# Hyena layer: both directions' filters on halves of the array, squares summed on GpSimd, filters placed among another round's products

## The reference, cut to what matters

```
def hyena_filters(length, w1, b1, f1, w2, b2, f2, w3):
    ...
    hid = jnp.sin(f1 * (feats @ w1 + b1))
    hid = jnp.sin(f2 * (hid @ w2 + b2))
    h = (hid @ w3).astype(jnp.float32).reshape(length, HY_ORDER, HY_DIRS, HY_W)
    h = h * jnp.exp(-t * decay)[:, None, None, :]
    return h * lax.rsqrt(jnp.sum(h * h, axis=0, keepdims=True) + EPS)

def hyena_layer(...):
    p = h @ w_in
    u = dwconv(p[..., :3 * HY_W], conv_w)
    v, x1, x2 = jnp.split(u, 3, axis=-1)
    filt = hyena_filters(...)
    z = x1 * long_conv(v, filt[:, 0, 0], filt[:, 0, 1], skip[0])
    y = x2 * long_conv(z, filt[:, 1, 0], filt[:, 1, 1], skip[1])
```

## Time and profile before

| | |
|---|---|
| runs | 4025.53 us median of 3 (4020.6 to 4029.58) |
| profiled execution, span | 4026.6 us, 72398 instructions |
| profiled execution beside the median | 1.1 us above it; the page gives no other time of its own |
| PE busy | 3681.6 us, 91% |
| DVE / ACT / POOL busy | 1654.0 / 1184.3 / 1366.7 us |
| Hyena rounds in the trace | 824.7 to 1319.8 us |

### The profile page before, as it was taken

The page is one execution under the profiler, slowest core; times in us unless marked ns, Lnnn a source line. Parts: engine busy times, 40 slices in busy tenths (PEclk is TensorE's granted clock), DMA queues, the critical chain, the costliest instruction groups (busy, mean ns, idle before and its releaser), DMA issues.

```text
span 4026.6 us, 72398 instructions
## 1 busy us (share of the span) xinstructions
PE 3681.6 (91%) x31788; PEld 2339.7 (58%) x31788; DVE 1654.0 (41%) x2930; ACT 1184.3 (29%) x2153; POOL 1366.7 (34%) x1215
## 2 busy tenths in 40 slices
PE   8997878999999998898899999899888888889998
PEld 3754565434444455565455555445666776748887
DVE  1345343234434122444433333643565656533344
ACT  3253222222212264432300000211556666420002
POOL 1320442002112022657433323334343434225444
PEclk9998787988898999989999999999999999989999
DMA  5430000621001211540111111132000000022222
GB/s 198 148 100 21 2 2 11 211 86 33 29 28 43 84 47 63 189 161 18 52 53 62 62 54 55 60 123 75 36 16 19 25 16 4 14 84 95 84 84 74
DMA packets 196419, 263.77 MB, mean 66 GB/s; under 512 B 6119, under 2 KB 151655, under 8 KB 194056
## 3 DMA queue, kind: packets, MB, share of 16 engines
q1 hardware_dynamic: 189024, 241.74, 18.0%
q10 hardware_dynamic: 7080, 17.40, 1.1%
HBM read 246.53 MB, written 12.58 MB: 64 GB/s over the span
## 4 chain that ended last, share of the span: by engine, by line
PE 50%; ACT 5%; DVE 4%; issue 3%; POOL 1%; DMA 0%; ACTq 0%; DVEq 0%; SPq 0%; POOLq 0%
PE ps L238 40%; PE ps L3123 2%; PE ps L771 2%; ACT mem L848 1%; PE ps L382 1%; PE ps L798 1%; PE ps L786 1%; PE ps L489 1%; DVE mem L829 1%; PE ps L3642 1%; POOL mem L3425 0%; PE ps L3650 0%; ACT mem L858 0%; PE ps L498 0%; ACT mem L3058 0%
## 5 line engine op out<-in xcount | busy, mean ns | idle before, releaser
L238 PE MATMUL ps<-mem 64*64 64x64 f32 (+4 forms) x25184 | 2690.3, 302 | 155.4 <-POOL mem L3026 29.0
L238 PEld LDWEIGHTS ps<-mem 64*64 64x64 f32 (+1 forms) x25184 | 1742.8, 155 | 1111.1 <-issue 578.2
L3026 POOL TENSOR_TENSOR mem<-mem 128x256 f32<-128x256 f32 (+1 forms) x264 | 226.0, 868 | 357.9 <-ACT mem L3535 178.8
L866 POOL TENSOR_SCALAR mem<-mem 128x768 f32<-128x768 f32 (+2 forms) x128 | 219.0, 1723 | 197.6 <-DVE mem L832 197.6
L2267 ACT ACTIVATE mem<-ps 128x384 f32<-128x384 f32 (+1 forms) x80 | 35.6, 445 | 781.1 <-PE ps L238 738.8
L2254 POOL TENSOR_TENSOR mem<-mem 128x512 f32<-128x512 f32 (+1 forms) x80 | 100.2, 1252 | 443.2 <-PE ps L238 371.2
L596 POOL TENSOR_TENSOR mem<-mem 128x512 f32<-128x512 f32 (+1 forms) x72 | 75.2, 1060 | 431.7 <-ACT mem L591 428.6
L2278 DVE TENSOR_TENSOR mem<-mem,ps 128x384 f32<-128x384 f32 (+1 forms) x80 | 39.9, 499 | 417.3 <-PE ps L238 417.3
L3123 PE MATMUL ps<-mem 128*128 128x128 f32 x960 | 178.1, 303 | 31.2 <-DVE mem L3048 20.1
L3056 ACT ACTIVATE mem<-ps 128x256 f32<-128x256 f32 (+1 forms) x220 | 101.4, 461 | 200.0 <-PE ps L3123 199.5
L3048 DVE TENSOR_TENSOR mem<-mem,ps 128x256 f32<-128x256 f32 (+1 forms) x220 | 109.7, 514 | 122.7 <-PE ps L238 121.9
(11 more groups left out here) (336 smaller groups left out, 4126.9 us busy)
## 6 DMA issues: line engine op xcount, KB each, us to landing
mem<-i_mod_w SPq DMA_DIRECT2D x48, 1024.0 KB, 6.8
mem<-i_ffn_wg SPq DMA_DIRECT2D x22, 1024.0 KB, 5.1
mem<-i_ffn_wu SPq DMA_DIRECT2D x22, 1024.0 KB, 5.1
mem<-i_e_w_in SPq DMA_DIRECT2D x16, 1024.0 KB, 6.0
mem<-i_o_w_in SPq DMA_DIRECT2D x16, 1024.0 KB, 5.5
mem<-i_ffn_wd SPq DMA_DIRECT2D x16, 1024.0 KB, 5.2
mem<-i_e_mod_w SPq DMA_DIRECT2D x12, 1024.0 KB, 11.8
mem<-i_o_mod_w SPq DMA_DIRECT2D x12, 1024.0 KB, 6.9
```

The lines of the kernel that those rows point to most:

```text
L238: ins = e.h.matmul(out, l, r, start=(i == 0), stop=(i == n - 1))
L866: K.pool.h.tensor_scalar(w, w, stat(i, o, 1), None, MUL).then_inc(*nm.up(tag, i, o))
L3026: K.pool.h.tensor_tensor(m3(self.slot(l)), self.lraw, bm(C(K, f"cm{self.d}", l, 64), 2 * self.np), MUL).then_inc(*self.mk.up(key, l))
```

## The change

Filters of both directions are computed as a pair: the second layer of the filter network writes `h2` on 128 partitions (its weights are loaded twice side by side), the w3 of both directions lies on the two halves of the partitions of one tile `w3t`, and the two products of a pair use rows 0 to 63 and 64 to 127 of the array and two banks. The host lays w3 out so. `w3t` is `K.rows[1]`, outside the ring; the filters H are moved out of Y (to the end of memory and to the part of `yo` that is written last), so that they can be computed while Y is in use. The squares go to G, POOL adds the four blocks, and one product with ones per direction is left. Norm, sum and difference are done in two halves z. A round's filters are computed in the round before, in four steps tt. The spectra, turns and copies are written in another order on PE and ACT.

```
-        self.w = [m[0:33, 0:64], m[0:64, 64:128]]
+        self.w = [m[0:33, 0:64], m[0:64, 64:192]]
+        self.rows = [64, 128]
...
+    w3t = K.rows[1]
-    H = [Y[:, 0:4, :], Y[:, 4:8, :]]
+    H = [K.mem[:, MEM - 2048:MEM].rearrange("p (a b) -> p a b", b=512), yo[:, 4:8, :]]
+    sums_at = lambda it: 0 if it else 2
+    place = lambda tt, d: 2 * ((tt + 1) % 2) + d
+    spectrum = lambda f, c: 2 * ((f + 1) % 2) + c
...
+    def filters_pe(it, tt):
+        if tt == 0:
+            window[it], _ = K.take(kn(256))
+            K.spent(window[it], fl, it, 3, 1)
+            K.pe.wait_ge(*sa.at(1))
+            K.pe.wait_ge(*lw.at(it))
+        for d in range(2):
+            vacant(K, place(tt, d))
+        for d in range(2):
+            ins = K.pe.h.matmul(K.ps[place(tt, d)], h2[64 * d:64 * d + 64, tt * 128:tt * 128 + 128], w3t[64 * d:64 * d + 64, :], start=True, stop=True)
+            K.busy[place(tt, d)] = [(fl, (it, tt, d))]
+        ins.then_inc(*w3.up(it, tt))
...
+    def filters_pool(it):
+        for tt in range(1, 4):
+            for d in range(2):
+                K.pool.wait_ge(*sqr.at(it, tt, d))
+                if tt > 1:
+                    K.pool.wait_ge(*ad.at("squares", it, tt - 1, d))
+                K.pool.h.tensor_tensor(G[:, 4 * d, :], G[:, 4 * d, :], G[:, 4 * d + tt, :], ADD).then_inc(*ad.up("squares", it, tt, d))
+    def sums_pe(it):
+        for d in range(2):
+            vacant(K, 2 + d)
+            K.pe.wait_ge(*ad.at("squares", it, 3, d))
+            K.pe.h.matmul(K.ps[2 + d], C(K, "ones"), G[:, 4 * d, :], start=True, stop=True).then_inc(*ss.up(it, d))
...
+    def norms_dve(it):
+        for z in range(2):
+            for d in range(2):
+                K.dve.wait_ge(*sqr.at(it, "r", d))
...
+                h = H[d][:, 2 * z:2 * z + 2, :]
+                K.dve.h.tensor_tensor(h, h, bm(G[:, 4 * d + 1, :], 2), MUL).then_inc(*fl.up(it, "n", d, z))
+    def sums_pool(it):
+        for z in range(2):
...
+            K.pool.h.tensor_tensor(HS[:, part, :], H[0][:, part, :], H[1][:, part, :], ADD).then_inc(*hs.up(it, z))
...
+        for tt in range(4):
+            filters_pe(0, tt)
+        for it, hf, o in rounds:
+            for x, t in enumerate(early[it]):
+                if x == sums_at(it):
+                    sums_pe(it)
+                conv_pe(it, t)
+            products(it, 0)
+            products(it, 1)
+            turned(it, 0)
+            turned(it, 1)
+            products(it, 2)
+            turned(it, 2)
+            turned(it, 3)
+            products(it, 3)
+            forward(it)
+            ahead = (lambda tt: filters_pe(it + 1, tt)) if it < 3 else (lambda tt: None)
+            ahead(0)
+            conv_pe(it, ("x", 2))
+            ahead(1)
+            inverse(it, 0, 1)
+            ahead(2)
+            conv_pe(it, ("x", 3))
+            ahead(3)
+            inverse(it, 2)
+            inverse(it, 3)
...
+            K.sp.wait_ge(*(w3.at(it - 1, 3) if it else K.sig("mod_turn", "pe").at("mod_b0", 20)))
+            K.sp.h.dma_start(w3t, I["w3"][:, o, hf * 512:hf * 512 + 512]).then_inc(*lw.up(it, by=16))
```

More of the change, by code:

```diff
@@ L1946, in long_convolutions @@
     rounds = [(hf * 2 + o, hf, o) for hf in range(2) for o in range(2)]
[L1947 to L1950, removed]
+    early = {it: ([("u", j) for j in range(4)] if o == 0 else []) + [("x", 0), ("x", 1)] for it, hf, o in rounds}
     order = {}
     for it, hf, o in rounds:
-        for part in tiles[it]:
-            for t in part:
-                order[it, t] = len(order)
+        for t in early[it] + [("x", 2), ("x", 3)]:
+            order[it, t] = len(order)
@@ new lines, in conv_pe, with conv_act @@
+    def conv_pe(it, t):
+        c = order[it, t]
+        b = 4 + c % 2
+        if t[1] % 2 == 0:
+            cur[0:2] = K.take(kn(256))
+        n, s = cur
+        vacant(K, b)
+        group(K.pe, K.ps[b], ((s[:, k, (t[1] % 2) * 128:(t[1] % 2) * 128 + 128], hap(k, 0, NX)) for k in range(KT)), KT).then_inc(*lin.up("hc", c))
+        K.busy[b] = [(pd, (c,))]
+        if t[1] % 2:
+            K.spent(n, lin, "hc", c)
+    def conv_act(it, t):
+        c = order[it, t]
+        K.act.wait_ge(*zero.at(1))
+        K.act.wait_ge(*lin.at("hc", c))
+        if c >= 2:
+            K.act.wait_ge(*cv.at(c - 2, 2))
+        K.act.h.activation(pad[c % 2][:, 1:NX + 1], K.ps[4 + c % 2], ACT.Copy).then_inc(*pd.up(c))
@@ L2067, in pe, with turned, forward @@
+        def turned(it, j):
+            b = 2 + j % 2
+            vacant(K, b)
+            K.pe.wait_ge(*fo.at(it, j, 1))
+            for i in range(4):
+                ins = K.pe.h.transpose(K.ps[b][:, i * 128:(i + 1) * 128], fold[j % 2][:, i * 128:(i + 1) * 128], C(K, "ident"))
+            ins.then_inc(*tu.up(it, j))
+            K.busy[b] = [(ut, (it, j))]
+        def forward(it):
             K.pe.wait_ge(*ut.at(it, 3))
@@ new lines, in inverse @@
+        def inverse(it, *js):
+            for j in js:
+                vacant(K, 6 + j % 2)
+            for i in range(2):
+                for f in range(4):
+                    c = i ^ odd(f)
+                    K.pe.wait_ge(*ad.at(it, f, c))
+                    for j in js:
+                        ins = K.pe.h.matmul(K.ps[6 + j % 2][:, 256 * i:256 * i + 256], Y[:, 4 * c + f, j * 128:(j + 1) * 128], Fi[:, c, f, :], start=f == 0, stop=f == 3)
+                        if f == 3 and i:
+                            ins.then_inc(*iv.up(it, j))
+                            K.busy[6 + j % 2] = [(mx, (it, j, 1))]
```

375 lines of the change are left out of this document (175 added, 200 removed).

## The result

| | before | after |
|---|---|---|
| runs of the comparison, median | 4023.07 us of 4 | 3899.56 us of 4 (3895.11 to 3903.02) |
| ratio | | 0.9698, 95% interval 0.9681 to 0.9715 |
| profiled span | 4026.6 | 3901.6 |
| the Hyena rounds, first filter product to first gate product | 495.04 | 373.96 |

What follows compares the result with a forecast made beforehand. TensorE (PE) was taken to bound the kernel, busy 3681.6 of 4026.6 us. The terms take the Hyena layer from 495.1 to 381.1 us, 114 less, giving a median of 3911.5 (forecast 3911); range 3896 to 3938.

Steps and rivals of the forecast that it cites:

- Step 1: Four filter stages, one ahead of each Hyena round, leave PE's path, with the slab's DMA wait: -124.8 us.
- Step 2: First round's filters still stand alone with nothing to hide them; first convolution at 836.5: +11.8 us.
- Step 3: Rounds 1 to 3: 12 filter pairs among other products, 1.0 us each plus two row-count changes of 0.2: +17 us.
- 4 ones-products: Since POOL sums the squares, 32 ones-products become 8, at 0.86 us each: +7 us.
- Step 5: PE's waits at turns, copies and inverse go, -15 us; lower clock outside the filter stages, -12 us.
- Step 6: Seams between rounds: other products hide the filter chain, 3 us of room; POOL and DVE disturbing each other: +2 us.
- A: Chain at the seam shows: PE waits and the clock falls, 24 us over three seams, time 3935; chance 0.16.
- B: Pairs don't overlap (29 instead of 17 us), first convolution at 841: +16 us, time 3928; chance 0.12.
- D: 64-row products pull TensorE's clock down for the rest of the layer: +340 - 114 us, time about 4250; chance 0.02.
- C: Better: pairs at 10 us, first convolution at 834, no lower clock, no collision: -14 us, time 3898; chance 0.10.

Runs made afterwards that it cites:

- the four parts undone: Changed kernel with pairs on the same rows, pairs together at the seam, eight ones-products without POOL's additions, old order: rounds 449.93 us, time 3978.71, ratio 0.9892.

## Why the prediction was right, step by step

The forecast was -114 us for the rounds; -121.1 came. Its terms, against what each measured:

| step | forecast | measured |
|---|---|---|
| 1 filter stages leave | -124.8 | -124.8, taken from before's own trace |
| 2 first filters alone | +11.8 | +10.7 (827.86 to 838.54) |
| 3 twelve pairs | +17 | +15.1 (0.86 + 2 x 0.20 each) |
| 4 ones-products | +7 | +6.9 (943.96 to 945.68, four times) |
| 5 waits, and the clock outside the stages | -15 and -12 | -15.0 and about -14.6, some 12 of it clock |
| 6 the seam | +2 | +2.8, at another place |
| not in the sum | | about -2.2 |

Step 1 was counted once and stands by construction; only the whole tests it. The experiments split the gain otherwise, by edit: 76 us for the four parts undone, 45 for the structure around them.

Step 2: right to 1.1 us, with the last two pairs at the lower clock (3.78 us) as worked out.

Step 3: the mechanism held. The 0.2 for each change was right. The factor from attention's pairs, 0.60, was too pessimistic: without the changes a pair is 0.86 against 1.72, a factor of 0.50. Rows 9 have changes of their own at both ends, and these were counted twice: the next product starts 1.49 us after 1699.71, which is four of the eight records, 1.29, and 0.2. The Trainium skill (TensorEngine Tiling, Tiling Modes) warns of a drain at each change of mode; in this trace a change costs 0.2 us, 5 us for all 24, and would not have spoken against scattering, which is worth 26.

Step 5: the waits went to the last tenth. Busy time outside the stages fell by 14.6: L238's records are busy 11.1 us less (290.9 to 279.8), the turns 1.4 (9.7 to 8.3) and the inverses 2.1 (59.4 to 57.3). The prediction had taken it from L238 alone, called all of it clock and kept 3 us for the start. Read from the granted clock it was smaller and ended at nothing: 0.97, 0.96, 0.97 and 0.96 over the 355.1 busy us between the stages of the kernel before are 12 us, and behind 838.54 the changed kernel has 1.00. So the -12 for the clock came out because a start that was too high (15) and an allowance that was not needed (3) cancel: luck; the other 2.6 us of shorter records, and the 2.2 of the last row, I can't place.

Step 6: the summed halves came 12.7 and 16.1 us after the last inverse; I had 12.2 and 14.5, and needed were 15.5 and 17.2. So the room was 2.8 and 1.1 us. The rule of the Trainium skill (SBUF — State Buffer, Who interferes with whom), that two such instructions of DVE and GpSimd go one after the other, gave 16.9 for the second half: it was the better estimate, and the trace comes near it. A norm (1.23 alone) and the first half sum (2.17 in its shortest case) took 2.98 us together from 953.70 to 956.68, where one after the other would be 3.40; the tap (0.75) and the second half sum took 2.72 from 957.85 to 960.57, against 2.92. But rule and prediction both looked at the sum, and PE didn't wait there. The delay went on through DVE's queue to the join of product 0. The step that was wrong is "needed at 17.2": the need of the bank of product 0, later on the same queue, was not worked out. The allowance of 2 us, made for POOL's sum, covered most of the 2.8 by luck.

Of the rivals, A (a wait at the seam that also pulls the clock down) came in a small form: a wait of 1.4 us, twice, behind which the granted clock stayed at 1.00 (965 to 975). B is refuted by 1.06 us a pair and by the first convolution at 838.54, 10.7 us after the first filter product. D is refuted, for pairs among dense products, by the clock row of 1.00 over a window with three pairs. C's time, 3898 (the range starts at 3896, which no sum of the prediction gives), is nearest to the 3899.6 measured, but of its parts only one holds, that almost no lower clock is left: its pairs at 10 are too cheap by their changes, and the collision was there. The number is 11 us off for two reasons: the rounds came 7 us shorter than their forecast, and what lies outside them 4, within its scatter.

## What to carry to other kernels

A step with a chain over several engines should be spread among another step's dense products, one link at a time, rather than given a stage of its own; the products' own time is the smaller part of what that saves, idle gaps and the clock behind them the larger. Where the order of an engine's queue is free, put a long product between each producer and its consumer: that alone was 23 us of the kernel before, not quite half of it clock. When a cover is worked out, follow the helping engines' queues up to the next bank or buffer that PE wants back, not only to the value that the step produces.

## What the runs showed of the hardware

- Two products on rows 0 to 63 and 64 to 127, 32 bits wide and 512 columns: 1.06 us a pair against 1.91 on the same rows. The difference is one whole product (0.86 us).
- A change between 64 and 128 rows: 0.2 us at the upper clock. Whatever stands between two changes is 0.2 us longer than its records at 0.431: the pair (1.06 for 0.86), the pair on the same rows (1.91 for 1.72), the convolution (7.08 for 6.89), the single product of the earlier trace rows (1.05 for 0.86).
- Three gaps of 1.27, 0.74 and 0.69 us, with eight short products between them, were followed by a granted clock of 0.72 over the next 6 us (0.51 in the earlier trace rows); over four rounds the clock cost about 7 us beside gaps of 10.8. A gap of 1.38 us behind turns and 20.6 us of full products was followed by 1.00; one of 1.37 us behind three 64-row products, in the kernel before, by the lower level. Which difference between the two decides was not tried.
- DVE beside POOL, both on operands in SBUF: an operation of 1.23 us took up to 3.02, one of 0.75 took 2.37, and POOL's own varied from 2.17 to 2.91.
